# Rests of the weight chunks on GpSimd: two instructions of 512 elements a partition instead of one of 1024, in 160 more chunks

## The reference

```python
# first block
mix = jnp.einsum('bse,ed->bsd', concatenate([o_a, o_b]), w_o[i])
h = h + rmsnorm(mix, g_post_mix[i])
v_ = rmsnorm(h, g_pre_mlp[i])
a = jax.nn.relu(jnp.einsum('bsd,df->bsf', v_, w_up[i]))
ff = jnp.einsum('bsf,fd->bsd', a * a, w_down[i])            # D_FF = 4096
h = h + rmsnorm(ff, g_post_mlp[i])
gate = jax.nn.sigmoid(jnp.einsum('bsd,de->bse', h, w_ple_gate[i]) + b_ple_gate[i])
h = h + rmsnorm(gate * ple, g_post_ple[i])
# second block, each of 2 layers
x = x + mix @ w_out[l]
h2 = rms_norm(x, norm2_g[l])
x = x + jnp.square(jax.nn.relu(h2 @ w_ff1[l])) @ w_ff2[l]
```

## Time and profile before

| what | value |
|---|---|
| median of three runs | 2741.99 us (2739.61 to 2743.61) |
| the profiled execution itself | 2745.7 us |
| its span, first to last instruction | 2743.8 us |
| mean granted TensorE clock | 0.975 of full speed |
| TensorE matmul busy | 2639.7 us (96%) |
| VectorE busy | 1587.9 us (58%) |
| ScalarE busy | 1099.5 us (40%) |
| GpSimd busy | 1036.1 us (38%) |
| DMA, mean over the span | 78 GB/s |

### The profile page before, as it was taken

The page is one execution under the profiler, slowest core; times in us unless marked ns, Lnnn a source line. Parts: engine busy times, 40 slices in busy tenths (PEclk is TensorE's granted clock), DMA queues, the critical chain, the costliest instruction groups (busy, mean ns, idle before and its releaser), DMA issues.

```text
span 2743.8 us, 44509 instructions
## 1 busy us (share of the span) xinstructions
PE 2639.7 (96%) x16872; PEld 2339.0 (85%) x16872; DVE 1587.9 (58%) x2494; ACT 1099.5 (40%) x1840; POOL 1036.1 (38%) x666
## 2 busy tenths in 40 slices
PE   7998999999989999999999999999999999999998
PEld 5787778888789998888999999989987777788888
DVE  5665423224489885443375664598883453566665
ACT  4445423223442333442345543333334342454443
POOL 2121444444334322112456544443321113565564
PEclk9998999999999999999999999999999999999999
DMA  5220233323222211111322221222111012332222
GB/s 153 65 86 24 69 102 95 97 92 96 73 68 93 67 53 64 38 32 41 122 86 100 100 93 62 91 93 78 55 56 55 31 39 71 125 105 93 92 101 85
DMA packets 61760, 215.30 MB, mean 78 GB/s; under 512 B 8144, under 2 KB 8144, under 8 KB 61584
## 3 DMA queue, kind: packets, MB, share of 16 engines
q1 hardware_dynamic: 48128, 169.43, 19.1%
q10 hardware_dynamic: 13088, 42.18, 4.6%
q0 software_dynamic: 368, 1.23, 0.1%
HBM read 210.65 MB, written 2.16 MB: 78 GB/s over the span
## 4 chain that ended last, share of the span: by engine, by line
PE 55%; issue 17%; DVE 12%; POOLq 6%; DVEq 5%; POOL 3%; ACT 1%; ACTq 0%
PE ps L702 13%; PE ps L703 13%; PE ps L704 13%; POOLq L615 6%; DVE arena L1945 2%; PE ps L925 2%; PE ps L926 2%; PE ps L927 2%; PE ps L1133 2%; DVE ps L2548 2%; POOL wl L613 2%; POOL dl L628 2%; PE ps L685 2%; DVEq L2537 1%; PE ps L1108 1%
## 5 line engine op out<-in xcount | busy, mean ns | idle before, releaser
L613 POOL TENSOR_TENSOR wl<-stage,wh 128x512 fp32r<-128x512 f32 (+1 forms) x476 | 813.7, 1724 | 1601.9 <-ACT wh L1271 1600.2
L702 PE MATMUL ps<-Uh,wh 128*128 128x264 f32 (+1 forms) x2640 | 895.8, 339 | 26.1 <-DVE Ul L1951 9.1
L703 PE MATMUL ps<-Ul,wh 128*128 128x264 f32 (+1 forms) x2640 | 865.8, 328 | 0.0
L704 PE MATMUL ps<-Uh,wl 128*128 128x264 f32 (+1 forms) x2640 | 863.5, 327 | 0.0
L1271 ACT ACTIVATE wh<-stage 128x1024 fp32r<-128x1024 f32 x318 | 336.9, 1060 | 985.1 <-PE ps L704 977.6
L702 PEld LDWEIGHTS ps<-Uh,wh 128*128 128x128 f32 x2640 | 503.5, 191 | 88.6 <-issue 16.3
L704 PEld LDWEIGHTS ps<-Uh,wl 128*128 128x128 f32 x2640 | 502.1, 190 | 43.1
L703 PEld LDWEIGHTS ps<-Ul,wh 128*128 128x128 f32 x2640 | 504.2, 191 | 40.4 <-issue 2.6
L2548 DVE SCALAR_TENSOR_TENSOR ps<-arena,v,ps 128x528 f32<-128x528 f32 x232 | 167.8, 769 | 8.3
L628 POOL TENSOR_TENSOR dl<-dstage,dh 128x512 fp32r<-128x512 f32 x112 | 144.7, 1311 | 51.5 <-ACT dh L1357 49.0
L925 PE MATMUL ps<-sumh,dh 128*128 128x256 f32 (+1 forms) x448 | 128.0, 286 | 10.2 <-DVE H L2159 7.6
(11 more groups left out here) (367 smaller groups left out, 4909.0 us busy)
## 6 DMA issues: line engine op xcount, KB each, us to landing
stage<-w SPq DMA_DIRECT2D x318, 512.0 KB, 3.5
dstage<-w_down ACTq DMA_DIRECT2D x56, 512.0 KB, 4.3
arena<-bias_rows ACTq DMA_DIRECT2D x16, 448.0 KB, 5.2
arena<-w_mla ACTq DMA_DIRECT2D x8, 384.0 KB, 3.0
H<-xT SPq DMA_DIRECT2D x8, 256.0 KB, 6.7
out<-H ACTq DMA_DIRECT2D x8, 256.0 KB, 2.8
arena<-pT SPq DMA_DIRECT2D x1, 512.0 KB, 8.8
arena<-causal POOLq DMA_DIRECT2D x1, 320.0 KB, 3.3
```

The source lines that it names most:

```text
L613: rest = pool.tensor_tensor(wl[:, j, cols], stage[:, j, cols], wh[:, j, cols].bitcast(F32), ALU.subtract)
L702: pe.matmul(dst, w_lead, tok.part(a_lead, h), start=(k == 0), stop=False)
L703: pe.matmul(dst, w_lead, tok.part(a_rest, h), start=False, stop=False)
L704: mm = pe.matmul(dst, w_rest, tok.part(a_lead, h), start=False, stop=(k == len(acts) - 1))
```

## The change

The default number of pieces in both helpers of GpSimd's program goes from 1 to `PIECES`, which is 2. The calls that gave `PIECES` before are as they were. The calls without it now make two instructions of 512 elements a partition: the first feed-forward and gate (line 641, 72 chunks), `w_out` (line 651, 16 chunks), the halved groups (line 657, 56 chunks) and the last group of layer 0 (line 664, 16 chunks).

```diff
@@ -605,7 +605,7 @@
-            def rest_of_chunk(j, pieces=1):
+            def rest_of_chunk(j, pieces=PIECES):
 
                 pool.wait_ge(w_lead_ready, n.next(w_lead_ready))
                 for piece in range(pieces):
@@ -614,7 +614,7 @@
                 rest.then_inc(w_split, 1)
                 pool.drain().then_inc(stage_free[j], 1)
 
-            def rest_of_weights(count, pieces=1):
+            def rest_of_weights(count, pieces=PIECES):
```

## The result

| | median of the runs | mean | runs | mean granted clock |
|---|---|---|---|---|
| changed kernel, first comparison | 2747.95 us | 2747.7 us | 20 | 0.9748 |
| kernel before, beside it | 2742.53 us | 2742.4 us | 20 | not listed |

A forecast was written before the change was run, and what follows sets the result against it. TensorE, busy 96% of the span, was taken as the bound, so only its waits count. Terms +0.6 + 0 - 0.8 + 1.0 - 0.3 = +0.5 us took the median from 2741.99 to 2742.5 us, range 2738.5 to 2747.0.

The forecast's parts named there:

- term C: Second norm, 761 us: `H` gets in after the first piece, so TensorE waits less; -0.8 us, bounds -1.1 and +0.1.
- term E: Ends of `w_out`, both layers: the sum gets between the pieces, `Ul` waits for the second; -0.3 us, bounds -0.9 and +0.3.
- everything else I cost at nothing: All other places: shorter VectorE waits hidden, later rests covered by the lead over TensorE, later loads harmless; 0 us.
- G: Behind the first norm, 718-759 us: a place the forecast did not see, so no term for it.
- term A: Start of first block's feed-forward, about 347 us: `HIDl` goes between the pieces, rest ends later; +0.6 us, bounds +0.14 and +1.0.
- rival 3: Upward units of the loops: TensorE's queue needs weights earlier than it seems; +9.6 us, 2752 us, chance 0.08.
- B: First norm, 700 us: first VectorE instruction gets in sooner, second waits for the second piece; 0, bounds -0.5 and +0.15.
- D: Seven group ends: longer GpSimd delays VectorE's sum and `H`, TensorE waits; 7 x 0.14 = +1.0 us.
- Rival 1: At the touched places VectorE isn't let in between pieces, issued back to back; +1.7 us, 2743.7 us, chance 0.15.
- rival 4: Half clock behind TensorE's idle places goes too; faster by more than 5.5 us, -8, 2734 us, chance 0.06.

The follow-up runs named there:

- last72: Kernel before with one chunk alone in two pieces, the last of the first block's 72, where the second norm begins (761 us); ratio 1.0000 (0.9988 to 1.0012).
- quiet: Changed kernel with 18 of 160 chunks whole again, those where TensorE waits behind them; 142 stay in two pieces; ratio 1.0000 (0.9991 to 1.0009).

## Why the prediction was wrong

- **The sum, "+0.5 us".** Slower was right; the size was not. The traces have 1.7 us of waits, and 1.6 of clock in a stretch that the change leaves alone. The steps that failed are term C (0.95 us of the difference), term E (0.6 us) and "everything else I cost at nothing" (0.2 us at G and the 1.6 us of clock); term A was too high by 0.5 us. Together that leads from +0.5 to the +3.3 of the traces. One by one:
- **C, "-0.8 us", was right alone and wrong in company.** `last72` gives -0.77. In the changed kernel it is +0.15. I took the arrival of `H` against GpSimd from the trace of before and asked only whether it fell within the first piece, not by how much: 1.11 us against a piece of 1.26. My upper bound, +0.1, was near this case and should have had more weight, with a margin of 0.15 us.
- **"Everything else I cost at nothing"** failed at G. I named 0.76 us as the tightest lead; at 722 us it was 0.20. It is one chunk of 160, for 0.2 us. It is not rival 3, by which TensorE would need the rest some 1.0 us ahead: here it starts 0.05 us behind it.
- **E, "-0.3 us", measured +0.3.** I saw that the sum goes between the pieces and `Ul` waits for the second, and credited 0.2 us. It loses the pair's 0.15 us instead: what VectorE's first instruction wins, the second gives back with the longer GpSimd on top. B came out at 0 (-0.02 to 0.05), right at the chunk of the earlier trace rows, but with 0.12 us for the chunk in front, which I left out, and the clock giving it back: partly luck.
- **A, "+0.6 us", measured 0.01 to 0.12.** VectorE was held through both pieces. The wait of TensorE for line 613 goes from 3.82 to 3.97 us, which is my lower bound of +0.14; the half clock behind it gives a little back.
- **D, "+1.0 us", measured 0.93 to 1.03.** Seven places, one free price: the part that a profile gives best.
- **Rival 1** (VectorE not let in: +1.7, 2743.7 us) has the sum of the touched stretches, but not for its reason. Only at A is VectorE not let in between the pieces. At B and E the first instruction is let in and the second pays it back; at C `H` comes when the second piece has begun; in the loops VectorE is let in 31 times of 32. I gave it 0.15 because the earlier trace rows showed an entry, and they were right about that. What they don't show is whether the arrival fits.
- **The clock.** I looked for it only behind the touched places, as rival 4, and not in stretches that the change leaves alone. I put it at nothing, without a row for it. The 1.6 us there put the mean past rival 1. What stays open is why the stretch from 1905 us is at half clock longer: it goes with a delay of TensorE of about 0.6 us in 20 traces, and no run shifts that stretch by a pure delay.
- **The median.** I took 2741.99, of 3 runs; the range's upper end was 5 us over it, and the changed kernel's runs alone spread from 2741.5 to 2753.0. (Added up from its own parts, the range would begin at 2738.0 and not at 2738.5; nothing hangs on that.)

## What to carry to other kernels

Splitting an instruction to let another engine in is worth what the arrival allows: list, for each place where the bound engine waits, when the other engine arrives within the piece, and count a margin under 0.2 us as a coin toss, since any other edit can shift it. Put the split only where a wait ends on it (four chunks in four pieces gave 0.9992 here, with an interval up to 0.9999, and 160 in two 1.0013). A forecast also needs every chunk near a wait, the one in front of it too. And when an effect is under 5 us, one trace of each kernel decides nothing: align several traces by the same matmul, and separate steps that recur in all from stretches whose clock differs.

## What was not expected of the hardware

- VectorE, waiting since 0.92 us after a pair's start, was not let in between its pieces (held 2.13 us at 348.33, and 2.10 to 2.12 in the other three traces of the changed kernel); at 0.96 us it was, in the earlier trace rows, and at about 1.18 us in the other 31 of 32.
- The same untouched work of 383 us took up to 3.0 us more or less between executions, with 34.1, 37.5 or 41.0 us of it at the lower clock; between such places two executions agree within 0.05 us.
- One wait of 1.0 us of TensorE at the end of a `w_out` brought half clock for 1.54 us of loss in `quiet`; waits at group ends, up to 1.6 us with four pieces, never did in 20 traces.
